# Group norm variances by products with a matrix of ones, and a first gather for four experts, in a two-block kernel

## What is computed

```python
def rwkv_group_norm(y, w, b):
    mu = jnp.mean(y, axis=-1, keepdims=True)
    var = jnp.mean((y - mu) ** 2, axis=-1, keepdims=True)
    yn = ((y - mu) * lax.rsqrt(var + RWKV_GN_EPS)).reshape(y.shape[0], y.shape[1], -1)
    return yn * w + b
...
    affinity = jax.nn.softmax((h @ w_router).astype(jnp.float32), axis=-1)
    gate_vals, tok_idx = lax.top_k(jnp.swapaxes(affinity, 1, 2), cap)
    xs = jax.vmap(lambda hb, ib: hb[ib])(h, tok_idx)
    hid = jax.nn.silu(jnp.einsum('becd,edf->becf', xs, w_gate)) * jnp.einsum('becd,edf->becf', xs, w_up)
    ye = jnp.einsum('becf,efd->becd', hid, w_down) * gate_vals[..., None].astype(h.dtype)
```

## Time and profile before

| | us |
|---|---|
| median of 3 runs (lowest to highest) | 2002.72 (1999.62 to 2007.18) |
| the profiled execution: its own time | 1994.0 |
| its span in the trace | 1992.1 |
| PE busy in the span | 1677.0 (84%) |
| DVE busy | 700.0 (35%) |
| ACT busy | 356.0 (18%) |
| POOL busy | 91.0 (5%) |

### The profile page before, as it was taken

One profiled execution on the slowest core, in us unless ns is written; L12 is line 12 of the kernel. 1 busy time (PEld: TensorE's weight loads), 2 busy tenths in 40 slices (PEclk: granted clock), 3 DMA queues, 4 the chain that ended last, 5 costly groups with the idle time before them and its releaser, 6 DMA issues.

```text
span 1992.1 us, 31970 instructions
## 1 busy us (share of the span) xinstructions
PE 1677.0 (84%) x14184; PEld 1141.1 (57%) x14184; DVE 700.0 (35%) x1247; ACT 356.0 (18%) x827; POOL 91.0 (5%) x94
## 2 busy tenths in 40 slices
PE   6999899987989676645655689998999899899997
PEld 2665458957975432211211257758994476669963
DVE  2006372463332300000000024564665244646663
ACT  2010212342231220000000022421010124310000
POOL 0000003402311000000000000000000000000000
PEclk8999898987999788778778889999999999999999
DMA  9431111040014599999999963213545532225440
GB/s 393 185 117 53 68 45 43 4 170 2 4 63 174 211 382 427 428 428 428 427 427 428 428 222 120 85 43 148 190 175 206 188 120 85 85 85 209 168 184 21
DMA packets 35593, 382.08 MB, mean 192 GB/s; under 512 B 6977, under 2 KB 10433, under 8 KB 12673
## 3 DMA queue, kind: packets, MB, share of 16 engines
q1 hardware_dynamic: 35458, 380.04, 47.6%
HBM read 378.98 MB, written 1.05 MB: 191 GB/s over the span
## 4 chain that ended last, share of the span: by engine, by line
PE 50%; DMA 11%; DVE 3%; ACT 1%; issue 1%; SPq 0%; DVEq 0%; ACTq 0%
PE psum L2761 14%; PE psum L1873 7%; PE psum L2832 7%; DMA arena<-in_w_moe 7%; PE psum L2168 6%; DMA weight_ring<-in_w_moe 5%; PE psum L2171 3%; PE psum L1848 3%; PE psum L2319 3%; PE psum L2309 1%; PE psum L1828 1%; PE psum L2288 1%; PE psum L2274 1%; PE psum L2197 1%; PE psum L2251 0%
## 5 line engine op out<-in xcount | busy, mean ns | idle before, releaser
L1873 PE MATMUL psum<-weight_ring,arena 128*32 128x512 f32 x640 | 142.0, 719 | 128.3 <-DMA arena<-in_w_moe 94.1
L1269 PE MATMUL psum<-arena 64*64 64x64 f32 x4608 | 150.8, 223 | 19.6 <-PEq L962 8.8
L2761 PE MATMUL psum<-arena 128*128 128x128 f32 x1408 | 165.2, 275 | 1.7 <-DVE arena L2965 1.7
L2761 PEld LDWEIGHTS psum<-arena 128*128 128x128 f32 x1408 | 161.1, 192 | 2.0 <-issue 2.0
L1269 PEld LDWEIGHTS psum<-arena 64*64 64x64 f32 x4608 | 143.2, 138 | 27.0 <-issue 22.8
L1873 PEld LDWEIGHTS psum<-weight_ring,arena 128*32 128x32 f32 x640 | 36.0, 129 | 205.5 <-issue 205.5
L2002 DVE COPY arena<-psum 128x512 f32<-128x512 f32 x16 | 11.1, 692 | 371.3 <-PE psum L1873 371.3
L1873 PE MATMUL psum<-arena 128*32 128x512 f32 x384 | 106.5, 715 | 33.6 <-DMA weight_ring<-in_w_moe 33.1
L2761 PE MATMUL psum<-arena,weight_ring 128*128 128x128 f32 x1056 | 129.8, 280 | 4.7 <-ACT arena L2879 2.6
L2761 PEld LDWEIGHTS psum<-arena,weight_ring 128*128 128x128 f32 x1056 | 125.2, 196 | 6.0 <-DVE arena L2969 2.8
L2168 PE MATMUL psum<-arena,weight_ring 128*128 128x256 f32 x512 | 123.6, 394 | 0.0
(11 more groups left out here) (497 smaller groups left out, 2226.2 us busy)
## 6 DMA issues: line engine op xcount, KB each, us to landing
weight_ring<-in_w_moe SPq DMA_DIRECT2D x60, 2048.0 KB, 20.2
arena<-in_w_moe SPq DMA_DIRECT2D x36, 2048.0 KB, 20.5
weight_ring<-in_w_in SPq DMA_DIRECT2D x23, 2048.0 KB, 8.7
weight_ring<-in_w_mod SPq DMA_DIRECT2D x12, 2048.0 KB, 8.0
weight_ring<-in_w_gate SPq DMA_DIRECT2D x12, 2048.0 KB, 7.6
weight_ring<-in_w_up SPq DMA_DIRECT2D x12, 2048.0 KB, 7.5
weight_ring<-in_w_down SPq DMA_DIRECT2D x12, 2048.0 KB, 7.6
weight_ring<-in_w_out SPq DMA_DIRECT2D x6, 2048.0 KB, 7.6
```

The lines of the kernel that those rows point to most:

```text
L1269: last = nc.tensor.matmul(K.ps[half[d], bank, column + HD * n:column + HD * n + HD], lhs(d, h), rhs(d, h), start=True, stop=True, skip_gro ...
L1873: last = nc.tensor.matmul(K.ps[strip(j), 4, :], xsT[:, k, CAP * e:CAP * e + CAP], ws[j][:, k, :], start=(k == 0), stop=(k == KT - 1), skip ...
L2761: last = nc.tensor.matmul(K.ps[:, bank, P * n:P * n + P], lhs, rhs, start=(n == 0 and k == 0 and name in ("m1", "m5", "m6")), stop=(k == 3 ...
```

## The change

In `outputs` the variances come from four products, each of the matrix of ones (block diagonal over the two directions) with the squares of a whole pair, 512 columns wide. The variance then stands on every partition of its direction, along the tokens, where y needs it. So `spread` goes; ScalarE takes four roots of 128x512 out of PSUM into the place of the squares, and VectorE four reciprocals of 128x512 in place, read from SBUF by the multiplication. Banks and the order of `partial`, `gates` and variances change with it. Behind the last Sqrt of `outputs` ScalarE computes one Exp of a constant into an unused place.

In `route_and_experts` the first gather covers 128 places (experts 0 to 3) and the second 384. Expert 0's four buffers are released by a no-op behind its products, and `widen`, with its copies on ScalarE, comes behind expert 0's down product.

```diff
--- before.py
+++ after.py
@@ -1509,11 +1508,11 @@
...
-    rstd_bank, gate_bank, fold_bank = (7, 4, 7, 4), (5, 6, 5, 6), (5, 7)
+    var_bank, gate_bank, fold_bank = (4, 6, 4, 6), (5, 7, 5, 7), (4, 6)
@@ -1559,18 +1558,15 @@
...
-                def spread(n):
-                    for j in range(2):
-                        for c in range(TT):
-                            for d in range(2):
-                                at = 2 * (2 * n + j) + d
-                                last = nc.tensor.matmul(K.ps[half[d], rstd_bank[n], T * j + P * c:T * j + P * c + P],
-                                                        rstd[:, c, at:at + 1].broadcast_to([P, HD]), K.ident,
-                                                        start=True, stop=True, skip_group_check=True)
-                    last.then_inc(rstd_made, 1)
+                def variance(n):
+                    pe.wait_ge(squared, n + 1)
+                    if n >= 2:
+                        pe.wait_ge(rooted, n - 1)
+                    nc.tensor.matmul(wide(var_bank[n]), K.head_ones, pair(sq, n), start=True, stop=True).then_inc(var_made, 1)
 
                 def fold(m):
-                    pe.wait_ge(z_ready, 3 + m)
+                    pe.wait_ge(z_ready, 2 + 2 * m)
+                    pe.wait_ge(rooted, 3 + m)
@@ -1614,36 +1610,27 @@
...
                 partial(2)
+                pe.wait_ge(sums_read, 1)
+                variance(0)
+                gates(0)
                 partial(3)
-                pe.wait_ge(sums_read, 1)
-                gates(0)
-                for n in range(4):
-                    pe.wait_ge(squared, n + 1)
-                    for j in range(2):
-                        for c in range(TT):
-                            h = 2 * n + j
-                            last = nc.tensor.matmul(K.ps[:, 4, 2 * H * c + 2 * h:2 * H * c + 2 * h + 2], sq[:, h, P * c:P * c + P],
-                                                    K.head_ones[:, ::HD], start=True, stop=True, skip_group_check=True)
-                last.then_inc(var_made, 1)
                 pe.wait_ge(sums_read, 2)
+                variance(1)
                 gates(1)
                 for m in range(4):
                     combine(m)
-                pe.wait_ge(rstd_ready, 1)
-                spread(0)
-                spread(1)
                 first, second = range(4), range(4, KT)
                 w0 = W.take(pe)
                 pe.wait_ge(gate_read, 1)
                 product(w0, 0, 0, first).then_inc(W.used, 1)
+                variance(2)
                 pe.wait_ge(z_ready, 1)
                 gates(2)
-                spread(2)
                 pe.wait_ge(gate_read, 2)
                 product(w0, 0, 1, first)
+                variance(3)
                 pe.wait_ge(z_ready, 2)
                 gates(3)
-                spread(3)
                 w1 = W.take(pe)
                 pe.wait_ge(gate_read, 3)
                 product(w1, 1, 0, first)
@@ -1698,19 +1685,26 @@
...
+                def take_root(n):
+                    act.wait_ge(var_made, n + 1)
+                    nc.scalar.activation(pair(sq, n), wide(var_bank[n]), ACT.Sqrt, bias=K.gn_eps[:, 0:1],
+                                         scale=1.0 / HD).then_inc(rooted, 1)
+
...
                 square(1)
                 keep_part(0)
                 square(2)
                 square(3)
-                for m in range(1, 4):
-                    keep_part(m)
-                act.wait_ge(var_made, 1)
-                nc.scalar.activation(root, K.ps[:, 4, 0:4 * H].rearrange("p (c h) -> p c h", c=TT), ACT.Sqrt,
-                                     bias=K.gn_eps[:, 0:1], scale=1.0 / HD).then_inc(rooted, 1)
+                keep_part(1)
+                keep_part(2)
+                take_root(0)
+                keep_part(3)
+                take_root(1)
                 for m in range(4):
                     act.wait_ge(gate_made, m + 1)
                     nc.scalar.activation(part[:, m, :], K.ps[:, part_bank[m], :], ACT.Copy).then_inc(gate_read, 1)
+                take_root(2)
+                take_root(3)
                 for t in range(TT):
@@ -1720,6 +1714,8 @@
...
                     nc.scalar.activation(scales[:, 2 + t:3 + t], ms[:, 2 + t:3 + t], ACT.Sqrt).then_inc(root_ready, 1)
+                    if t == 1:
+                        nc.scalar.activation(part[:, 0, 0:1], K.ones[:, 0:1], ACT.Exp)
                     act.wait_ge(turned, 2 * t + 1)
@@ -1738,16 +1734,16 @@
                 dve.wait_ge(g_sum_made, 1)
                 nc.vector.tensor_tensor(bonus, K.ps[:, 6:8, :].rearrange("p a (b t) -> p (a b) t", t=T), bonus,
                                         ALU.mult).then_inc(sums_read, 1)
-                dve.wait_ge(rooted, 1)
-                nc.vector.reciprocal(rstd, root).then_inc(rstd_ready, 1)
                 dve.wait_ge(sums_read, 2)
                 dve.wait_ge(centred, 4)
                 for n in range(4):
-                    dve.wait_ge(rstd_made, n + 1)
+                    dve.wait_ge(rooted, n + 1)
+                    nc.vector.reciprocal(pair(sq, n), pair(sq, n)).then_inc(rstd_ready, 1)
+                    dve.wait_ge(rstd_ready, n + 1)
                     for j in range(2):
                         h = 2 * n + j
                         last = nc.vector.scalar_tensor_tensor(y[:, h, :], y[:, h, :], K.dup_vecs[:, 0, h:h + 1],
-                                                              K.ps[:, rstd_bank[n], T * j:T * j + T], ALU.mult, ALU.mult)
+                                                              sq[:, h, :], ALU.mult, ALU.mult)
                     last.then_inc(rstd_used, 1)
@@ -1814,18 +1810,20 @@
...
+    slices = (slice(0, P), slice(P, NE * CAP))
...
         def gather(part):
-            cols = slice(256 * part, 256 * part + 256)
+            cols = slices[part]
...
                 for t in range(TT):
-                    last = nc.tensor.matmul(K.ps[:, d % 4, 0:256], K.h2[:, t, P * d:P * d + P], sel[:, t, cols],
+                    last = nc.tensor.matmul(K.ps[:, d % 4, cols], K.h2[:, t, P * d:P * d + P], sel[:, t, cols],
                                             start=(t == 0), stop=(t == 1))
                 last.then_inc(gathered, 1)
@@ -1874,6 +1872,9 @@
...
             last.then_inc(gu_made, 1)
+            if e == 0:
+                pe.wait_ge(gu_made, 1)
+                nc.tensor.nop().then_inc(W.used, 4)
             if e:
                 scatter(e - 1)
@@ -1881,12 +1882,11 @@
...
             for c in range(4):
                 last = nc.tensor.transpose(K.ps[:, 5, P * c:P * c + P], gu[:, P * c:P * c + P], K.ident)
-                if c == 0:
+                if e and c == 0:
                     last.then_inc(W.used, 4)
             last.then_inc(gu_turned, 1)
             if e == 0:
                 gather(1)
-                widen()
             wd = [W.take(pe) for _ in range(2)]
@@ -1901,13 +1901,15 @@
             last.then_inc(down_made, 1)
             pe.wait_ge(down_made, e + 1)
             nc.tensor.nop().then_inc(W.used, 2)
+            if e == 0:
+                widen()
         scatter(NE - 1)
@@ -1925,18 +1927,19 @@
...
             if e == 0:
                 keep_gathered(1)
+            act.wait_ge(down_made, e + 1)
+            if e:
+                act.wait_ge(y_made, e)
+            for n in range(2):
+                last = nc.scalar.activation(parts[:, n, :], K.ps[:, 6 + n, :], ACT.Copy)
+            last.then_inc(parts_kept, 1)
+            if e == 0:
                 for n in range(8):
                     t, q = n // 4, n % 4
                     act.wait_ge(wide_made, n + 1)
                     nc.scalar.activation(scatter_to[:, 4 * q:4 * q + 4, P * t:P * t + P],
                                          K.ps[:, n % 4, :].rearrange("p (k t) -> p k t", t=P),
                                          ACT.Copy).then_inc(wide_kept, 1)
-            act.wait_ge(down_made, e + 1)
-            if e:
-                act.wait_ge(y_made, e)
-            for n in range(2):
-                last = nc.scalar.activation(parts[:, n, :], K.ps[:, 6 + n, :], ACT.Copy)
-            last.then_inc(parts_kept, 1)
```

More of the change, by code:

```diff
@@ L1500, in outputs @@
     part, rows, gains, mix = A.temp(4, 512), A.temp(2, D), A.temp(2, D), A.temp(TT, D)
-    root, rstd = A.temp(TT, 2 * H), A.temp(TT, 2 * H)
     sums, ms, scales = A.temp(4), A.temp(4), A.temp(4)
@@ L1511, in outputs @@
     part_bank = (0, 2, 1, 3)
-    rstd_bank, gate_bank, fold_bank = (7, 4, 7, 4), (5, 6, 5, 6), (5, 7)
+    var_bank, gate_bank, fold_bank = (4, 6, 4, 6), (5, 7, 5, 7), (4, 6)
     mixed = lambda t: K.ps[:, 2 * t:2 * t + 2, :].rearrange("p a b -> p (a b)")
     with nc.cleanup_on_exit():
-        mean_made, centred, squared, var_made, rooted, rstd_ready, rstd_made, rstd_used, z_ready, folded = (
-            K.sem("o_" + n) for n in ("mean_made", "centred", "squared", "var_made", "rooted", "rstd_ready", "rstd_made",
```

(4 more changed lines are left out.)

## The result

| | before | changed |
|---|---|---|
| median of the first comparison, us | 2001.74 (4 runs, 1999.62 to 2007.18) | 1985.38 (4 runs, 1983.22 to 1989.25) |
| ratio, 95% interval | | 0.9916 [0.9891, 0.9942] |
| second comparison | 1998.7 (31 runs) | 1988.65 (8 runs), 0.9944 [0.9924, 0.9963] |
| third comparison | 1996.18 (19 runs) | 1984.43 (8 runs), 0.9945 [0.992, 0.9969] |
| span of the profiled execution | 1992.1 | 1983.0 |

The ratio of the first comparison, with four executions of each, gives a gain of 16.8 us (0.0084 x 2001.7); the two later ones, with more executions, give 11.2 us (0.0056 x 1998.7) and 11.0.

A forecast was written before the change was run, and what follows sets the result against it. Experts were taken as paced by their weight stream, whose start the serial part before sets. First release 12.3 us earlier, but the second (7.8 + 4.2 slack, less a restart) limits the gain to 11.3: 2002.7 - 11.3 = 1991.4 us, range 1987 to 1998.

The forecast's parts named there:

- group norm: TensorE's group norm stage: 10.4 us of products removed, 3.6 added, so the stage ends 6.8 us earlier.
- Exp ahead: Start of routing: a dummy Exp loads the table beforehand in ScalarE's idle time, gaining 1.04 us.
- first gather and eviction: Before expert 0: gather of 128 columns takes 6.2 us for 9.54, plus 0.1 for the smaller eviction.
- first release in all: Expert 0's buffers: freed 12.3 us earlier, from 6.8 + 1.04 + 3.4 + 1.1.
- second release: Buffers freed after expert 1's products: 7.8 us earlier; with 4.2 us of slack it sets the stream, 12.0 at best.
- load of expert 2: Weight load on which expert 2 waits: lands 10.5 to 12.0 us earlier, 11.3 taken as the middle.
- the restart: Weight queue running dry for an instant before expert 2: restarting it costs up to 1.5 us.
- the cover on VectorE: Group norm: the last pair is ready 3.3 us or more before the second fold needs it.
- Rival 1: Second release comes later still: two to four microseconds lost, gain 8 to 10, 1993 to 1995 us; chance 0.17.
- Rivals 2 and 5: VectorE reciprocals in the group norm: 6 us each, 1997.0 us, chance 0.08; or 9 us each, 2009.0, chance 0.03.
- Rival 3: Exp table load stays at routing: 1.04 us less gain, 1992.4 us; chance 0.06.
- rival 4: First gather wholly at high clock: the first release holds the gain, 13 to 14 us; chance 0.06.

The follow-up runs named there:

- e6: Changed kernel with expert 0's four buffers released as before, by the first transpose; 1391.4 us from the group norm stage's start to the end (changed 1394.0).
- e8: Changed kernel with the widening back ahead of expert 0's down product; 1394.6 us from the group norm stage's start to the end (changed 1394.0).
- e7: Changed kernel with two gathers of 256 places; 1391.8 us from the group norm stage's start to the end (changed 1394.0).
- e13: Changed kernel run a third time, unaltered, against the kernel before; ratio 0.9945 [0.992, 0.9969].
- e2: Changed kernel run again, unaltered, with more rounds beside the kernel before; ratio 0.9944 [0.9924, 0.9963].
- e11: Changed kernel with GpSimd's additions and products held back until VectorE finishes the pairs; 1392.2 us from the group norm stage's start to the end (changed 1394.0).
- e10: Changed kernel with each of the four wide reciprocals made twice; 1407.9 us from the group norm stage's start to the end (changed 1394.0, before 1404.4).

## Why the prediction was right or wrong

| step of the prediction | forecast, us | measured, us |
|---|---|---|
| group norm | 6.8 | 6.8 (82.35 - 75.56) |
| Exp ahead | 1.04 | 1.03 |
| first gather and eviction | 3.4 | 3.1 (to the first products, 10.29 to 7.17) |
| first release in all | 12.3 | 12.0 |
| second gather | +3.4 | +3.4 |
| second release | 7.8 | 7.6 (139.98 to 132.41) |
| load of expert 2 | 10.5 to 12.0 | 11.0 (pair of profiles); 8.7 to 11.9 over all pairs |
| expert 15 | 11.3 | 10.4; 9.0 to 10.5 over all pairs |

**Wrong was the absolute time and its range.** The step that failed is "in those of the median 2002.7 - 11.3 = 1991.4", with a range of 1987 to 1998. It took the median of three runs as fixed, though the profiled execution of the same kernel took 1994.0. In the larger comparisons that followed the medians of before are 1996.2 to 1998.7, with single runs from 1987 to 2004. The range held the bounds of the gain and the rivals, but not this: with a gain of 11.3 and a base between 1994 and 2003 the low end had to be below 1983. The measured 1985.4 is that gain from a base of 1996.7, within those later medians. The chance given to faster was right in direction; the first sample's interval [0.9891, 0.9942] begins its gains at 11.6 us.

**The mechanism was right.** The clock held, the table stayed through the block, the second release set the stream, the queue ran dry for a moment. The Trainium skill (ScalarE activation tables: per-element evaluation and per-set limits, "Table sets in the compiler and the runtime") says that table loads are placed per block; read as a load in each block, one should have stood at routing, and no trace of the changed kernel has it. The gain behind expert 2 isn't quite kept: 11.0 becomes 10.4 in the first pair. Mis-sized was what the queue needs. The prediction let load 14 be issued up to 2.6 us before load 13 lands (731.9 against 734.5); in e6 and e8, at 3.3 and 4.2 us, a gap still opened (6.1 and 6.2 us behind load 13), and in e7, at 5.4, none did. And the restart was to cost "up to 1.5 us", but in e13 load 14 landed 7.9 us behind load 13, 3.0 more than in a full queue, while in e2 it was 0.4 more. So expert 2 starts at 144.9, 145.8 and 147.7 with the same issue time within 0.2 us, and one repeat gained 8.7 us there, under the forecast's 10.5. Why it varies was not tried.

**Mis-sized too was the cover on VectorE**: 3.3 us forecast, 1.3 found. The prediction watched semaphores and not what GpSimd does at the same time; with GpSimd out of the way, in e11, the 3.3 us are there. Moving the operand of the multiplication from PSUM to SBUF exposed it to GpSimd, and cost 4.1 us that happened to be hidden. The Trainium skill (SBUF — State Buffer, "SBUF: two separate sides") says that a VectorE operation with two inputs in SBUF and a GpSimd operation that reads SBUF exclude each other for the whole instruction. The trace agrees: the two multiplications took 2.48 and 2.58 us, each to the end of one GpSimd operation, and the prediction should have drawn on it. **Rival 1** didn't occur in its own way, since the second release came as forecast, though one repeat kept only 9.0 us at expert 15. **Rivals 2 and 5** were excluded by 3.35 us, and e10 shows that they were real. **Rival 3** was excluded by the missing load, **rival 4** by a gather of 6.53 us.

## What to carry to other kernels

When a stream of loads is the bound, list the releases one after another with the time by which each is needed: moving work past one of them pays only until the next becomes late, and here releasing every expert's buffers before the scatter closed the gap that the rearrangements of the first expert had opened (1.5 to 2.6 us at expert 15, seen in traces). Compare kernels from the start of the changed stage if what comes before it scatters, and put the scatter of the base into the range of an absolute time.

## What was not expected of the hardware

Two multiplications on VectorE with all operands in SBUF took 4.97 us beside GpSimd's work on 128x1024 and 0.88 without it, while a reciprocal out of SBUF beside it kept its 3.35; those that read one operand from PSUM took 0.87 beside it before the change. TensorE's waits in e10, the longest of 7.24 us before the second fold, brought the granted clock from 0.99 to 0.50, and routing started 3.0 us later than the delay of that fold accounts for. Load 14, 2 MB issued 1.9 to 2.0 us before the queue's last load landed, took 7.3, 8.2 and 9.9 us to land in three executions of the same program (e2, changed, e13). And equal programs differed by 5.9 us within their first 50 us, in rows that look like TensorE's low clock, of which the granted clock shows a part.
